# A scan step with its normalisations in another place, and a first feed-forward block of eight channel groups

## What is computed

```python
# layer 0: gated linear attention, then a gated MLP with a causal width-3 convolution
q, k, v, r, gl = split(rmsnorm(x) @ w_in)
log_a = log_sigmoid(gl @ w_gate_up + b_gate) / 16
k_dec = k * exp(tot - cum)                       # cum: sum of log_a within a chunk, tot: its end
S_c   = exp(tot_c) * S_{c-1} + k_dec_c^T @ v_c   # one state per chunk and head
o_c   = q_c @ S_c                                # every frame of chunk c reads S_c
x = x + (rmsnorm_per_head(o) * gn * silu(r)) @ w_out
g, u = split(rmsnorm(x) @ w_up)                  # 2816 channels each
x = x + (silu(causal_conv3(g)) * u) @ w_down
# layer 1: a short gated convolution in place of the attention, the same MLP, a last rmsnorm
```

## Time and profile before

| | us |
|---|---|
| median of 3 runs (lowest, highest) | 1510.04 (1509.15, 1588.21) |
| the profiled execution | 1510.03 |
| span of its slowest core, core 1 | 1508.7 |
| spans of the eight cores | 1499.3 to 1508.7 |
| PE busy (share of the span) | 1446.9 (96%) |
| DVE, ACT busy | 808.8 (54%), 649.0 (43%) |
| one convolution pass (L504, L506), one silu (L510), one product (L511) | 1.28, 1.06, 1.22 |
| a load of ACT's function table (ahead of L510, L333 or L391, where the functions change) | 1.28 |

### The profile page before, as it was taken

How to read it: one execution, slowest core, us unless ns; L and a number is a source line. 1 busy time by engine, 2 the same in 40 slices (tenths; PEclk the granted TensorE clock), 3 DMA queues, 4 the chain that set the end, 5 groups by cost and what they waited for, 6 DMA issues and landing times.

```text
span 1508.7 us, 19954 instructions; the slowest of 8 cores (1499.3 to 1508.7 us)
## 1 busy us (share of the span) xinstructions
PE 1446.9 (96%) x6960; PEld 659.1 (44%) x6960; DVE 808.8 (54%) x992; ACT 649.0 (43%) x1071; POOL 68.3 (5%) x102
## 2 busy tenths in 40 slices
PE   4799999987999999999999899999999999999998
PEld 2344444433444444444444344444444444444443
DVE  2336714765555445545567455566555345545567
ACT  4456656765442044204455333344543034304454
POOL 1000000000100000000000000100010000000000
PEclk9899999998999999999999999999999999999999
DMA  8931110171613033302347323355333022202214
GB/s 180 202 127 22 22 43 13 30 91 42 92 29 56 0 43 50 52 10 38 49 71 97 51 35 42 57 92 90 57 57 56 1 43 50 41 16 43 49 42 182
DMA packets 120338, 89.12 MB, mean 59 GB/s; under 512 B 62495, under 2 KB 107824, under 8 KB 120240
## 3 DMA queue, kind: packets, MB, share of 16 engines
q0 software_dynamic: 54336, 49.34, 22.8%
q1 hardware_dynamic: 65904, 38.50, 10.4%
HBM read 114.09 MB, written 8.39 MB: 81 GB/s over the span
## 4 chain that ended last, share of the span: by engine, by line
PE 90%; ACT 3%; DVE 3%; DMA 2%; issue 2%; SPq 0%; ACTq 0%; DVEq 0%
PE PS L478 39%; PE PS L406 27%; PE PS L729 11%; PE PS L555 10%; ACT xtm L331 1%; DMA xnb_u<-xtm 1%; DMA X<-x 1%; DVE gl_s_u L827 1%; PE PS L777 1%; PE PS L819 1%; DVE PS L875 1%; PE PS L784 1%; PE PS L848 0%; PE PS L765 0%; DVE xtm L351 0%
## 5 line engine op out<-in xcount | busy, mean ns | idle before, releaser
L406 PE MATMUL PS<-wring_u,ffn_h_u 128*128 128x512 bf16 x1408 | 304.9, 379 | 0.0
L478 PE MATMUL PS<-xna_u,wring_u 128*128 128x512 bf16 x1344 | 293.8, 380 | 2.6 <-DVE ffn_h_u L511 2.6
L478 PE MATMUL PS<-xnb_u,wring_u 128*128 128x512 bf16 x1344 | 292.0, 379 | 0.0
L413 DVE TENSOR_TENSOR X<-X,PS 128x512 f32<-128x512 f32 x256 | 173.9, 686 | 158.0 <-PE PS L406 157.9
L497 ACT ACTIVATE ffn_a_u<-PS,vecs_sb 128x1024 f32<-128x1024 f32 x88 | 98.0, 1114 | 277.5 <-PE PS L478 277.5
L406 PEld LDWEIGHTS PS<-wring_u,ffn_h_u 128*128 128x128 bf16 x1408 | 137.8, 98 | 166.1
L478 PEld LDWEIGHTS PS<-xna_u,wring_u 128*128 128x128 bf16 x1344 | 131.8, 98 | 162.6 <-issue 5.2
L478 PEld LDWEIGHTS PS<-xnb_u,wring_u 128*128 128x128 bf16 x1344 | 131.5, 98 | 158.6
L510 ACT ACTIVATE ffn_a_u<-ffn_a_u 128x1024 f32<-128x1024 f32 x88 | 93.0, 1057 | 229.6 <-DVE ffn_a_u L506 229.6
L511 DVE TENSOR_TENSOR ffn_h_u<-ffn_a_u,PS 128x1024 bf16<-128x1024 f32 x88 | 107.5, 1222 | 125.3 <-ACT ffn_a_u L510 116.5
L504 DVE SCALAR_TENSOR_TENSOR ffn_a_u<-ffn_g_u,vecs_sb,ffn_a_u 128x1024 f32<-128x1024 f32 x88 | 113.0, 1285 | 79.5 <-ACT ffn_g_u L503 74.3
(11 more groups left out here) (97 smaller groups left out, 1047.1 us busy)
## 6 DMA issues: line engine op xcount, KB each, us to landing
wring_u<-f_w_up POOLq DMA_DIRECT2D x14, 1024.0 KB, 11.7
wring_u<-f_w_down POOLq DMA_DIRECT2D x44, 256.0 KB, 7.3
X<-x SPq DMA_DIRECT2D x16, 512.0 KB, 9.4
out<-X SPq DMA_DIRECT2D x16, 512.0 KB, 2.6
wring_u<-f_w_up POOLq DMA_DIRECT2D x8, 768.0 KB, 10.3
wring_u<-b_w_in POOLq DMA_DIRECT2D x12, 512.0 KB, 8.0
X<-a_w_out SPq DMA_DIRECT2D x8, 512.0 KB, 14.9
gamma<-gam SPq DMA_DIRECT2D x5, 512.0 KB, 8.6
```

What stands on the lines that cost most here:

```text
L406: ins = nc.tensor.matmul(self.PS[:, b, :], Y[:, k, yi * 128:(yi + 1) * 128], w[k].ap[:, n * 512:(n + 1) * 512], start=(k == 0), stop=(k == ...
L413: lambda: nc.vector.tensor_tensor(xs, xs, self.PS[:, b, :], ALU.add))
L478: ins = nc.tensor.matmul(self.PS[:, bank, :], blk.ap[:, kc, q * 128:(q + 1) * 128], self.xn(kc, hh * 8 + t * 4), start=(kc == 0), stop=(kc ...
```

## The change

Two things are edited. In a scan step the first normalisation's ACT part stands ahead of `g_cast(1)`, and a second one behind `g_read(g-1)`. And the first feed-forward block takes eight groups over the first half of the tokens, then all eight over the second half; its weights come in pieces of 2, 2 and 4 groups, the third issued when the output weights of the attention are free, and the wait for the last tile of XN ahead of it is gone. The list `left` is written anew: the parts for tiles 12 and 13 leave the end of step 15 and go into units 2 and 3, those for 14 and 15 into unit 4 (`gla_last`); the statistics of tile 15 come ahead of the projection of tile 14.

```diff
-                nb = min(4, gn - jj)
+                nb = min(8 if first and left else 4, gn - jj)
-                if l == 0 and j0 == 4:
-                    self.pool.wait(self.bXN[NTT - 1].w)
-                pieces = [2, 2] if first and left else [nb]
+                pieces = [2, 2, 4] if first and left else [nb]
...
+                        if len(pieces) > 1 and hh == 0 and jb == 4:
+                            while left:
+                                left.pop(0)()
+                            self.attention_done()
+                            load(pieces[2], self.ring)
+                            left += self.gla_last()
                         if hh == 1 and first:
                             while left:
                                 left.pop(0)()
                             first = False
-                            self.attention_done()
...
             self.g_v(g, 1)
+            for what in norms.get(g, [])[:1]:
+                self.norm_a(*what)
             if i >= 1:
                 self.g_cast(1)
-            for what in norms.get(g, []):
-                self.norm_a(*what)
...
                 self.norms_b()
-                self.norm_a("f_norm0", g - 3)
-                self.norm_a("f_norm0", g - 2)
                 return
...
                 self.g_read(g - 1)
+            for what in norms.get(g, [])[1:]:
+                self.norm_a(*what)
...
-        return [lambda: self.g_gated(g - 1), b, lambda: self.g_read(g), lambda: self.g_out(g - 1),
-                lambda: self.g_stats(g), lambda: (self.g_gated(g), b()), nothing, lambda: (self.g_out(g), n(14)),
-                b, nothing, lambda: n(15), b]
+        return [lambda: self.g_gated(g - 1), nothing, lambda: self.g_read(g), lambda: self.g_stats(g),
+                lambda: self.g_out(g - 1), lambda: self.g_gated(g), nothing, lambda: self.g_out(g),
+                nothing, lambda: (n(12), n(13)), nothing, b, b]
+
+    def gla_last(self):
+        def n():
+            self.norm_a("f_norm0", NTT - 2)
+            self.norm_a("f_norm0", NTT - 1)
+        nothing = lambda: None
+        return [nothing, n, nothing, self.norms_b]
```

More of the change, by code:

```diff
@@ L236, in __init__ @@
         self.DEC = nc.alloc_sbuf_tensor("dec", [128, HEADS, T // CH], F32)
-        self.HAL = nc.alloc_sbuf_tensor("hal", [128, 4, 2], F32)
-        self.bHAL = [Buf("hal") for _ in range(4)]
+        self.HAL = nc.alloc_sbuf_tensor("hal", [128, 8, 2], F32)
+        self.bHAL = [Buf("hal") for _ in range(8)]
         self.base = nc.sbuf_base
@@ L445, in ffn, with load @@
                     self.ring.align()
-                if l == 0 and j0 == 4:
-                    self.pool.wait(self.bXN[NTT - 1].w)
-                pieces = [2, 2] if first and left else [nb]
+                pieces = [2, 2, 4] if first and left else [nb]
                 wg, wu = {}, {}
                 o = 0
-                for p in pieces:
-                    ring = self.ring0 if p < nb and o == 0 else self.ring
+                def load(p, ring):
+                    nonlocal o
                     g = ring.load(wup[:, :, (j0 + o) * 128:(j0 + o + p) * 128], 128, [KC, p * 128])
@@ L459, in ffn @@
                     o += p
+                for k, p in enumerate(pieces[:2]):
+                    load(p, self.ring0 if len(pieces) > 1 and k == 0 else self.ring)
                 for hh in range(2):
```

## The result

The changed kernel took 1534.96 us (median of five runs, 1533.25 to 1535.41) beside 1509.71 for the kernel before; the ratio is 1.0164, interval 1.015 to 1.0178. The forecast was 1505, its range 1496 to 1512. Some executions of most of the kernels have one die at a lowered clock for much of the run and take up to 280 us more; they count in no ratio and in no comparison of undisturbed cores, but in the medians over all eight cores that are given for chips B, C and E.

A forecast was written before the change was run, and what follows sets the result against it. Everything to gain was put in 240 to 400 us: 21.6 us of PE waits and a few us of halved clock. Scan minus 4.5, units 0 and 1 minus 3.4, units 2 and 3 plus 2.8 gave 1505, range 1496 to 1512.

The forecast's parts named there:

- scan: Scan steps: shorter waits with one normalisation moved ahead of the state's copy, minus 4.5 us in sum.
- units 0 and 1: First feed-forward units: earlier start, the 2.7 us bank wait replaced by one of 1.1; minus 3.4 us, bounds minus 6.3, minus 0.7.
- units 2 and 3: Unit 2's silu comes behind two normalisations, so u of unit 3 waits 4.4 us, not 2.6; plus 2.8 with halved clock.
- weights: Third piece, two 1 MB loads: landed 12.3 and 19.8 us after unit 2's start, cost nothing, cover 4.9 shrinking to 1.6.
- Steps 10 to 14: Scan: the keys' waits for ACT to empty the decay's banks go, minus 3.2 and minus 2.0 us.
- In the first half ... a projection lies ahead of the read: Scan steps with one normalisation: the projection covers the state's copy, so the move costs nothing; uncovered, up to 1.8 us a step.
- Step 9, minus 1.0: Scan step without a projection ahead of its read: read ends at 250.7, statistics come at 252.5 instead of 253.5 us.
- Step 15, plus 1.7: Uncovered scan step: copy and read come 1.3 us later, wait grows from 2.0 to 3.3, plus 0.4 of halved clock.
- A: Third piece of weights lands late and PE waits in unit 4; 18 us of waiting, 1523 us; chance 0.08.
- B: Clock stays up because the scan's waits ahead of its first fall are gone; 1499 us; chance 0.2.
- C: Copy behind a normalisation holds up the read in every two-normalisation step and the bank wait returns; 1509 us; chance 0.17.
- D: ACT stays blocked 2.7 us at each change of tables, not 1.3, by the page's drain; 1506 us; chance 0.05.

The follow-up runs named there:

- the kernel with the banks from unit 2: Changed kernel, but the feed-forward units get all eight PSUM banks from unit 2, not unit 4: 1504.27 us, ratio 0.9962 to the kernel before.
- copy first without cover, banks from unit 2 and even pieces: Changed kernel with state copy first in steps 1, 9, 15, eight banks from unit 2, weights in 2, 2, 2, 2 groups: 1491.65 us on chip B's undisturbed cores.
- the thin loads: Changed kernel, but weight loads into the ring after the first 48 slots move an eighth of their bytes: 1502.45 us, ratio 0.9948 to the kernel before.

## Why the prediction was wrong

**The step that failed** is the first: "they are alike, so core 1, the slowest, stands for all", with the reading that PE is busy "at full clock" from 400 us to the end carried over to the changed kernel. No term and no rival had the clock behind 400 us in it, and the 25 us lie there and on no other place: 0.81 for 162 us on pairs of cores. The bound for a loss by over 2% looked only at late weights.

**What brings 0.81 on** stays open. Shown: the changed kernel can run without the long stretch (19 runs of it on A and D with every core at a mean of 0.983 or more); the kernel before has the short stretches in its trace on chip E and lowered mean clocks on B and C; and most stretches begin beside loads of weights. Not settled: why in the first measurement the lowered pairs came in 5 of 5 runs of the changed kernel, with none in four of five of before. (Three of those five are the runs of the first table, so at most two stand beside the changed kernel in time; the contrast is weak.) For a part of this order: the long stretch was seen only in traces of kernels that are the changed one up to that place, in two measurements, both times at 389 us, near the end of the 2 MB and four down loads that this change puts beside units 2 to 4 (DMA share 1.07 and 1.20 in the 3 us ahead). Against it as the cause: on A and D a lone pair of lowered cores came in 1 of 29 runs of such kernels (48 of before had none), and core 0 of the first measurement had a share of 1.47 at the same place and stayed at 1.00. That this order makes a fall likelier where a chip is near its limit is a conjecture.

**The terms.** Measured from the decay of step 1, which lies ahead of what was moved, to the down projection; once on core 1, and once as the difference of the medians over the cores (the six without the long stretch, the eight of before):

| us | forecast | core 1 | all undisturbed cores |
|---|---|---|---|
| scan | −4.5 | −1.1 | −3.7 |
| units 0 and 1 | −3.4 | −4.5 | −2.8 |
| units 2 and 3 | +2.8 | +2.2 | +3.9 |
| weights | 0 | 0 | 0 |
| sum | −5.1 | −3.4 | −2.7 |

On five chips the changed kernel was 3.2 to 4.4 us under the kernel before. The columns differ because in the kernel before the clock falls at other places on other cores: on core 1 it falls in unit 3, at 385.5, and on none of the seven others, and in the scan core 1 has one fall where they have two. So core 1 did not stand for all in this layer either. That its sum is nearer to the forecast is luck. The bullets are for core 1, where no other is named.

- *Steps 10 to 14* came out: −4.3 at the keys of step 15, although 1.3 had been lost by step 9; so 5.6 was gained there, for 5.2 forecast.
- *"In the first half ... a projection lies ahead of the read"* is false for step 1: its read comes right behind the decay's matmuls. New wait 1.46, 1.6 of halved clock in the read and the keys behind it, less a wait of 1.13 that went: +1.9. I had read the order at step 14 and taken it for 13 steps.
- *Step 9, minus 1.0*, was +0.4. The read was late as foreseen (250.7), but I counted the 8 matmuls for the keys at 1.7; behind the wait they took 3.56. I had given the clock a price in step 15 and none here.
- *Step 15, plus 1.7*, was +2.3: the wait of 3.3 is right (3.32), its halved clock cost 1.1 (5.65 for 4.55), not 0.4.
- *Units 0 and 1*: the bank wait of 1.1 is there (0.99), the last projection's too (4.32 for "about 4.2"). The surplus of 1.1 is that projection at 5.19 for 6.33: the clock had risen sooner.
- *Units 2 and 3*: u at plus 15.3 for 14.95, the wait 4.7 for 4.4; but the clock behind it cost nothing more than before, so +2.2. On the other cores the wait of 2.6 had no fall behind it before and the wait of 4.7 has one now, so +3.9: "the halved clock behind it from 1.8" held for core 1 alone.
- *The third piece*: landed 11.5 and 18.8 behind its issue, for 11.9 and 18.6; PE never names it. That the cover is thin was shown by the kernel with the banks from unit 2.
- *Rivals*. A did not happen. B: one half, the clock in the last projection. C took place in step 9, and in step 1, which has one normalisation; not in 11, 13 and 14. D: unit 3 would have stood at plus 16.4; it is at 15.3. The drain that the Trainium skill gives in "ScalarE: Activation LUTs", What ACT_TABLE_LOAD costs, is not seen in this trace: a table load of 1.28 us starts at 347.44, 0.02 behind the end of the silu, and the logarithm starts at 348.73.

**A better kernel** came of the misses: copy first without cover, banks from unit 2 and even pieces stand 17.9, 17.3 and 16.9 us under the kernel before on the undisturbed cores of three chips, 1.1%; over all eight cores it was 13.9 and 16.7 under it on C and E. I have no ratio on a chip with all cores undisturbed. Its core 4 on chip C:

```profile
240.00:400.00 160.00, 146.67 (x816) 67.53 (x815) 103.72 (x153) 108.58 (x192) 9.17 (x12) 0.99 0.45 63
```

146.7 us busy at a clock of 0.99, where core 1 of before had 138.4 at 0.95 (core 4 of before: 139.0 at 0.96).

## What to carry to other kernels

A move in one engine's queue must be priced at every step that it touches, and first at those without cover: read the order of the consumer there, not at the step that prompted the change. Behind each new wait of PE count the matmuls that follow at the lower clock too; of 1.46 us of waiting in step 9 came 1.7 us of slower keys. Read such prices on more than one core: the same wait of 2.6 us cost 1.6 us of halved clock on core 1 and nothing on seven others. When the time of a kernel moves by a per cent or more and the local terms do not add up to it, look at each core's clock before looking for a cause in the code, and run the same kernel on another chip beside the kernel before. When an edit is to take something away from a place, look in the trace whether it is gone there before the result is read: the thin loads began 200 us later than meant.

## What the runs showed of the hardware

- TensorE has a third granted clock here, 0.81, between the halved and the full one (76 matmuls in 20 us for 95). It falls on both cores of a pair at one time (388.8 and 388.6, 389.5 and 389.8), while the other six go on at 1.00 with the same work.
- It comes in two forms: 23 to 30 stretches, most of 5 to 10 us, on the four cores of one die (chips B, C and E, every kernel traced there; on chip A up to three of them on the cores of one die), and one of 162 us (twice). The first costs 24 to 38 us of span (medians, chips C and B), the other 25 to 31.
- The short ones mostly begin beside loads of weights (22 of 26, where a third would be chance): DMA share 1.13 in the 3 us ahead, 0.81 behind; 30 us with a share of 0.12 stay at 1.00 with PE just as busy. Loads beside dense matmuls are not enough: at 1.47 and 1.24 other cores stayed at 1.00. The Trainium skill ("TensorE: Matmul & The Clock Gate", in Part 1, the note on the peak-current limiter) says that a whole die goes to 13/16 of its clock once a third core of it runs dense matmuls, and stays there while the load lasts. The level agrees (0.81). The rest does not: all eight cores ran dense matmuls, and on chips A and D most runs had a mean clock of 0.983 or more on every core; a pair fell alone; and the level was left with PE still fully busy.
- Two loads of 1 MB beside dense matmuls, issued 0.9 us apart with four smaller ones behind them, took 11.5 and 18.8 us to land on core 1; over 18 cores of six traces of the changed kernel it was 8.4 to 12.3 and 15.2 to 19.4. A cover of 1 or 2 us can't be placed by one core's number.
